# Feed-forwards: the low part of the inner activations is subtracted by GpSimd instead of VectorE

## The reference, cut to what matters

```python
def swiglu(h, w_gu, w_down):
    a, b = jnp.split(h @ w_gu, 2, axis=-1)
    return (jax.nn.silu(a) * b) @ w_down
# D_FF = 2816; per layer l:
x = x + 0.5 * mx[2] * swiglu(modulate(rms_norm(x, ...), mx[0], mx[1]), w_ffn1_gu[l], w_ffn1_down[l])
...
mx = jnp.split((silu_c @ w_ada[l] + b_ada[l])[:, None, :], 9, axis=-1)
```

## Time and profile before

| | |
|---|---|
| median of 3 runs | 2378.61 us (2377.94 to 2378.79) |
| profiled execution | 2378.87 us |
| its span, first to last instruction | 2377.1 us |
| mean granted TensorE clock in it | 0.985 of full speed |
| TensorE busy | 2289.9 us |
| VectorE busy | 1590.3 us |
| ScalarE busy | 887.6 us |
| GpSimd busy | 241.5 us |

### The profile page before, as it was taken

One profiled execution on the slowest core, in us unless ns is written; L12 is line 12 of the kernel. 1 busy time (PEld: TensorE's weight loads), 2 busy tenths in 40 slices (PEclk: granted clock), 3 DMA queues, 4 the chain that ended last, 5 costly groups with the idle time before them and its releaser, 6 DMA issues.

```text
span 2377.1 us, 33029 instructions
## 1 busy us (share of the span) xinstructions
PE 2289.9 (96%) x13198; PEld 1951.3 (82%) x13198; DVE 1590.3 (67%) x2898; ACT 887.6 (37%) x1507; POOL 241.5 (10%) x321
## 2 busy tenths in 40 slices
PE   6988989999999999999999999999999999998998
PEld 6878878988888777777888888888888898798998
DVE  5787886888877547875589866654333356876665
ACT  4444445422223444533322222332222234644443
POOL 1001012000102200012111111200000030021001
PEclk9999999999999999999999999999999999999999
DMA  7534534665643321222256565423222233254553
GB/s 264 168 126 159 169 126 143 217 217 174 221 172 123 116 69 65 67 84 98 91 195 240 201 212 205 140 80 107 93 94 98 93 111 105 98 170 141 188 184 119
DMA packets 97657, 341.31 MB, mean 144 GB/s; under 512 B 11312, under 2 KB 13488, under 8 KB 97120
## 3 DMA queue, kind: packets, MB, share of 16 engines
q1 hardware_dynamic: 74144, 254.46, 31.5%
q0 software_dynamic: 23360, 84.74, 11.0%
HBM read 338.11 MB, written 2.48 MB: 143 GB/s over the span
## 4 chain that ended last, share of the span: by engine, by line
PE 77%; DVE 13%; issue 4%; ACT 4%; POOL 1%; DMA 1%; POOLq 0%; DVEq 0%; ACTq 0%
PE PS L595 76%; DVE WL L1268 3%; ACT WH L965 1%; PE PS L916 1%; DVE NT L1277 1%; DVE HL L1277 1%; DVE JK L1278 1%; DVE AR L1278 1%; POOL ACC L1860 1%; ACT P L966 1%; DVE PJB L1277 1%; DVE CV L1277 1%; DMA RAW<-in_wst 0%; DVE P L1272 0%; POOL SS L1860 0%
## 5 line engine op out<-in xcount | busy, mean ns | idle before, releaser
L965 ACT ACTIVATE WH<-RAW 128x1024 fp32r<-128x1024 f32 (+3 forms) x498 | 511.5, 1028 | 977.3 <-PE PS L595 973.7
L595 PE MATMUL PS<-HH,WH 128*128 128x512 f32 (+1 forms) x2240 | 777.8, 347 | 11.1 <-DVE HL L1277 6.1
L595 PE MATMUL PS<-HL,WH 128*128 128x512 f32 (+1 forms) x2240 | 768.3, 343 | 0.0
L595 PE MATMUL PS<-HH,WL 128*128 128x512 f32 (+1 forms) x2240 | 768.1, 343 | 0.0
L1268 DVE TENSOR_TENSOR WL<-RAW,WH 128x1024 fp32r<-128x1024 f32 (+3 forms) x498 | 589.1, 1184 | 118.5 <-ACT WH L965 117.3
L595 PEld LDWEIGHTS PS<-HH,WH 128*128 128x128 f32 x2240 | 426.4, 190 | 74.4 <-DVE HL L1277 9.2
L595 PEld LDWEIGHTS PS<-HH,WL 128*128 128x128 f32 x2240 | 427.0, 191 | 52.5
L595 PEld LDWEIGHTS PS<-HL,WH 128*128 128x128 f32 x2240 | 427.3, 191 | 51.2
L595 PE MATMUL PS<-GH,WH 128*128 128x512 f32 (+1 forms) x776 | 271.2, 350 | 0.0
L595 PE MATMUL PS<-GL,WH 128*128 128x512 f32 (+1 forms) x776 | 270.2, 348 | 0.0
L595 PE MATMUL PS<-GH,WL 128*128 128x512 f32 (+1 forms) x776 | 270.1, 348 | 0.0
(11 more groups left out here) (220 smaller groups left out, 2791.6 us busy)
## 6 DMA issues: line engine op xcount, KB each, us to landing
RAW<-in_wst SPq DMA_DIRECT2D x436, 512.0 KB, 3.5
AR<-in_w_adaT POOLq DMA_DIRECT2D x144, 512.0 KB, 3.8
RAW<-in_wst SPq DMA_DIRECT2D x48, 384.0 KB, 3.0
BM<-rpb_rows POOLq DMA_DIRECT2D x48, 64.0 KB, 3.0
CB<-in_cc POOLq DMA_DIRECT2D x2, 1024.0 KB, 11.3
RAW<-in_wst SPq DMA_DIRECT2D x8, 256.0 KB, 2.7
RAW<-in_wst SPq DMA_DIRECT2D x4, 396.0 KB, 3.0
rpb_rows<-in_rpb POOLq DMA_DIRECT2D x2, 697.5 KB, 11.8
```

The lines of the kernel that those rows point to most:

```text
L595: return e.matmul(o, l, r, start=start, stop=stop)
L965: return e.activation(o, i, f, bias=bias, scale=scale)
```

## The change

VectorE's subtraction `GL = FT - GH` is taken out of its `evictions`, and GpSimd gets the same subtraction in its own, at the same place `V` of the list of steps. GpSimd waits there for ScalarE's rounding (`gh`). Those who waited for VectorE's signal `gl`, which are TensorE before the down products and ScalarE before the tanh of `ga`, now wait for GpSimd's. The whole diff:

```diff
@@ operand (TensorE)
             if un.buf == "G":
                 for s in halves:
-                    q.wait_ge(*vd.at("gl", l[0], PARTS[l[0]][l[1]][0] + kk, s))
+                    q.wait_ge(*gd.at("gl", l[0], PARTS[l[0]][l[1]][0] + kk, s))
@@ scalar_program, evictions, "ga"
                         if i >= 2:
                             for s in x.halves:
-                                q.wait_ge(*vd.at("gl", un.stage - 3, i - 2, s))
+                                q.wait_ge(*gd.at("gl", un.stage - 3, i - 2, s))
@@ vector_program, evictions, "gb"
                         stt(F, F, 0.5, P[:, 0:n], ALU.mult, ALU.mult).then_inc(*vd.inc("ev", d))
                         vd.same("gb", d)
-                        q.wait_ge(*ad.at("gh", d))
-                        tt(GL[:, slot(f, i), x.cols], F, GH[:, slot(f, i), x.cols].bitcast(f32), ALU.subtract).then_inc(
-                            *vd.inc("gl", f, i, x.halves[0]))
-                        vd.same("gl", f, i, x.halves[-1])
@@ pool_program, evictions
+                    elif x.kind == "gb":
+                        f = un.stage - 3
+                        q.wait_ge(*ad.at("gh", d))
+                        tt(GL[:, slot(f, i), x.cols], FT[:, i % 2, x.cols], GH[:, slot(f, i), x.cols].bitcast(f32),
+                           ALU.subtract).then_inc(*gd.inc("gl", f, i, x.halves[0]))
+                        gd.same("gl", f, i, x.halves[-1])
```

## The result

| | before | after |
|---|---|---|
| median | 2378.28 us (6 runs, 2376.19 to 2380.84) | 2393.33 us (6 runs, 2388.45 to 2395.25) |
| span of the profiled execution | 2377.1 us | 2393.5 us |
| mean granted clock in it | 0.985 | 0.981 |

The ratio is 1.0054, with a 95% interval of 1.0042 to 1.0067: 10 to 16 us slower. The median of after is 15 us higher. 2386.0 had been forecast, with 2377 to 2394 as range. So the sign was right and the range held, though by 0.7 us only, where single executions lie up to 5 us from their median; the size came out at about twice the forecast of 7.4 (15 us by the medians, 13 by the ratio).

A forecast was written before the change was run, and what follows sets the result against it. TensorE was taken as the bound, busy 2289.9 of 2377.1 us. Losses 3.3 + 4.8 + 0.8 + 2 + 1 = 11.9 less gain 4.5 gave +7.4 on 2378.9: 2386.3, for the median 2386.0, range 2377 to 2394.

The forecast's parts named there:

- What is removed: 98 subtractions leave VectorE; gain mainly from TensorE's waits at the start of f = 0, 4.5 us (1 to 8).
- Rival B: Faster: the waits of f = 0 vanish, the clock stays up, CB lands in time; 2372 us at best, chance 0.08.
- Price of a subtraction: On GpSimd a 512-column subtraction takes 1.28 us instead of 0.69, plus the rest of a VectorE operation already begun.
- Step 1: Start of f = 2: CB issued at 1186.8 behind a subtraction, landing at 1191.65, so ScalarE's tanh starts 3.4 us late.
- Steps 2 to 4: Start of f = 2: late CB delays VectorE, the first w_ada loads and a split; TensorE waits 3.3 us.
- the walk: The prediction's event-by-event trace of delays in f = 2, from the issue of CB to TensorE's waits.
- Step 5: First part of f = 2: rounds of GL, load, ada step and FT delay the sixth GL; TensorE waits 4.8 us (3 to 6).
- Step 6: Second part of f = 2: the same rounds average 11.1 us against TensorE's 11.2; wait 0.8 us (0 to 2), third part none.
- rival C: The circle of loads grows through the second and third part of f = 2; +19 us, 2398 us, chance 0.08.
- Step 7: The clock falls after TensorE's long waits in f = 2, costing 2 us (0 to 5).
- The other feed-forwards: f = 0, 3 and 5: later GL at ends of parts makes TensorE wait, 1 us in sum (0 to 2).

The follow-up runs named there:

- x8: Changed kernel, but only f = 0 has the subtraction on GpSimd, loads behind it; median 2379.1 us, ratio 0.9999 to the kernel before.
- x1: Changed kernel, but VectorE keeps the subtraction in f = 2; median 2380.7 us, ratio 1.0009 to the kernel before.
- x3: Changed kernel, all subtractions on GpSimd, but the next loads issued ahead of its wait for the rounding; median 2373.8 us, ratio 0.9985.
- x5: Changed kernel, but loads issued ahead of the subtractions at the start of f = 2 only; median 2384.1 us, ratio 1.0025.
- x7: As x3, but VectorE keeps the subtraction in f = 5; median 2372.9 us, ratio 0.9969 to the kernel before.
- x11: Changed kernel, but only f = 0 has the subtraction on GpSimd, with loads issued first; median 2376.0 us, ratio 0.9991.
- x2: Changed kernel, but only f = 2 has the subtraction on GpSimd; median 2396.6 us, ratio 1.0077 to the kernel before.
- x6: Changed kernel, but loads issued ahead of the subtractions everywhere except at the start of f = 2; median 2384.0 us, ratio 1.0015.
- x4: Changed kernel, but VectorE makes the subtractions and GpSimd only waits for the rounding, its DMAs behind that; median 2385.6 us, ratio 1.0031.
- x9: Changed kernel, but only the load of CB is issued ahead of a subtraction at the start of f = 2; median 2390.1 us, ratio 1.0056.
- x10: As x3, but each subtraction in f = 2 from the second inner tile on is made twice; median 2384.6 us, ratio 1.0030.

## Why the prediction was right or wrong

**What is removed: right in kind, too high.** Taken was a gain of 4.5 us (1 to 8). The waits at the start of f = 0 shrank from 4.55 to 1.79, the one at 433 vanished, the idle time in that stretch fell by 2.8, and by the marks the changed kernel stood 3.1 us ahead before f = 2. How much of the 3.1 is the change's own is open: the time up to the first wait of f = 0 runs from 406.0 to 412.3 over the thirteen profiled executions, and x8, with the change in f = 0 alone, shows no gain in its total. The fall of the clock after the first wait stayed (0.66 from 410 to 415 in both). Rival B needed it to go.

**Price of a subtraction: right.** With 512 columns GpSimd's took 1.26 to 1.34 us in 14 of 56 cases, which is the price of the row for the operation alone. It took 1.46 to 1.62 in 16 and 1.80 to 1.82 in 26, and I read what they have over 1.3 as GpSimd's own waiting for a VectorE operation that had begun. At the ends of parts in f = 3 the margin held.

**Step 1, CB: issue right, landing wrong.** GpSimd and the load at the start of f = 2, and its landing (DMA issues from 1150 to 1250), which answer to the earlier trace rows:

```profile
1182.20 1.47 POOL L1856 TENSOR_TENSOR GL<-FT,GH 128x256 fp32r<-128x256 f32 x1 [7.99 <-ACT GH L965]
1183.61 0.59 POOL L1956 DMA_DIRECT2D CB<-in_cc  x1
1197.94 1.29 POOL L1856 TENSOR_TENSOR GL<-FT,GH 128x512 fp32r<-128x512 f32 x1 [13.74 <-ACT GH L965]
1199.18 1.11 POOL L1950 DMA_DIRECT2D AR<-in_w_adaT  x2
```

```profile
CB<-in_cc POOLq DMA_DIRECT2D x1, 1024.0 KB, 7.6
```

Counted from the mark, it was issued at +21.3 (predicted 1186.8, +21.4). But the prediction kept the landing of 4.8 us, and it took 7.6. The versions that issue it early have 4.5 to 5.0 (x1, x3, x5 and x7 to x11), those that issue it six microseconds later, behind a subtraction, 7.6 to 7.9 (also x2, x6). Part of it may be the weight loads beside it: from issue to landing SyncE's queue moved 0.07 MB next to its 1.05 MB before, and 0.57 MB in the 7.6 us of after. But in x4, late and without a subtraction ahead, 0.79 MB were moved beside it and it took 6.0. The pieces of `w_ada` point the same way: from 1150 to 1250 their median was 3.8 us before and in x4, and 4.4 to 4.5 in the four versions that issue all or most of them right behind a subtraction (the changed kernel, x2, x5, x9). So that the late load takes longer is shown, and that it takes longest behind a subtraction; why is open. The prediction carried a landing time over to another moment without asking what else is moved then.

**Steps 2 to 4: one wait missed.** VectorE in after, which answers to the earlier trace rows:

```profile
1193.16 2.29 DVE L1277 SCALAR_TENSOR_TENSOR CB<-AR,CB 128x2048 f32<-128x2048 f32 x1 [7.78 <-ACT AR L965]
1195.37 1.22 DVE L1268 TENSOR_TENSOR WL<-RAW,WH 128x1024 fp32r<-128x1024 f32 x1
1196.50 0.68 DVE L1277 SCALAR_TENSOR_TENSOR FT<-FT,PS 128x512 f32<-128x512 f32 x1
1203.17 1.23 DVE L1278 SCALAR_TENSOR_TENSOR JK<-AR,CB 128x1024 bf16<-128x1024 f32 x1 [5.99 <-DMA AR<-in_w_adaT]
...
1205.47 1.22 DVE L1268 TENSOR_TENSOR WL<-RAW,WH 128x1024 fp32r<-128x1024 f32 x1
...
1248.41 0.68 DVE L1277 SCALAR_TENSOR_TENSOR FT<-FT,PS 128x512 f32<-128x512 f32 x1
1249.88 2.30 DVE L1278 SCALAR_TENSOR_TENSOR JK<-AR,CB 128x1024 bf16<-128x1024 f32 x1
```

FT of gb1 was foreseen at 1197.0 (it is 1196.5), the load at 1199.7 (1199.18), the first ada step at 1203.7 (1203.17), the split from 1206.0 (1205.47). But the walk named TensorE's wait for the second split only, 3.3 us. The split before it, at 1195.37, is late too: TensorE waits 2.03 for it. Together 6.32 in place of 3.3. The walk moved `CB` and its split and never asked when TensorE needs that split. The clock times agree, but the stage had begun 3.1 us earlier than the walk assumed: counted from the mark everything is late by the longer landing.

**Step 5, the circle: right, short by 3 us of 52.** From gb1 on, FT to FT was 16.4, 12.2, 13.8 and 9.5 us, against 16.4, 10.4, 12.8 and 9.1 foreseen: 51.9 against 48.7. Landings of the pieces went from 3.8 to 4.5 us (medians from 1150 to 1250). FT of the sixth tile came at 1248.41 (1245.8), `GL` ended at 1251.1 (1248.8), TensorE waited 4.61 (4.8): the extra 3 us of the circle were covered by the extra 3 us that TensorE had already waited. x5 and x6 show that circle and start each cost something by themselves.

**Step 6: too small.** The second part's wait is 3.22, for which 0.8 (0 to 2) stood. It went by averages, which don't hold the lengthened operations beside each subtraction. The third part has no wait over 0.4, as foreseen, so rival C is out.

**Step 7, clock: too small**, 5.1 us in f = 2 against 2, at the upper end of its 0 to 5. Both waits of over 4 us had the clock at half speed, as every one of 3.75 us or more has in the other versions' f = 2. Below that the length of a wait doesn't tell: at the 3.22 of after the clock stayed at 1.00 (1380 to 1390), at the 2.09 of x5 it fell (0.77 from 1365 to 1370).

**The other feed-forwards: 1 us foreseen.** f = 0 has a new wait of 0.85, f = 3 none over 0.4 for `GL`, f = 5 three, 1.89 together. Its stage took 201.9 to 203.1 us in the seven versions with GpSimd subtracting there, and 199.5 to 200.2 in the six without, so these waits are its cost of some 2 us; x7 takes them away. In the changed kernel it is 3.3, the rest a longer time at clock 0.50 behind the norm.

Sum of the errors: gain up to f = 2 too high by 1.4, start +3.0, first part -0.2, second part +2.4, clock and rest of f = 2 +2.4 (the 4.4 where 2 stood), f = 5 +2.3 (3.3 where 1 stood for three stages), stage of f = 3 -2.4. Of this last, half is the clock behind its norm (0.69 and 0.62 in the first windows of before) and half a matmul of 232.4 ns instead of 233.3, both chance as far as the runs tell. That is +8.9 on 7.4, or 16.3, against the 16.4 between the spans. It comes out by single executions, and chance terms of 1 to 2 us are in it.

**The range held in part by luck.** Its upper end counts 17 us of losses, while the bounds of its own terms add up to 3.3 + 6 + 2 + 5 + 2 = 18.3. And the start, the largest term after the first part, had no range at all: 3.3 stood in both ends, and 6.32 was measured.

## What to carry to other kernels

Before a wait is added to an idle engine, list the DMAs that stand behind it in its queue. Here a 1.3 us subtraction was harmless and a wait in front of the loads was not. The same work with the loads issued first turned 10 to 16 us of loss into a gain of 1 to 6 us (x3), and of 4.5 to 10 with VectorE keeping the subtraction in f = 5 (x7). And when a transfer moves, ask twice: when is it issued, and what else is being transferred then.

## What the runs showed of the hardware that I had not expected

- VectorE and GpSimd took turns by whole operations: 2.32, 2.31, then 1.21 us for the same kind of VectorE operation beside two subtractions of GpSimd (x10). VectorE's ada steps had means of 1385 and 1341 ns with GpSimd subtracting and 1218 and 1250 without (x4). Of 142 us that the change took off VectorE, 56.7 of it busy, the busy time shrank by 9.3.
- The load of 1 MB landed in 4.5 to 5.0 us or, issued 6 us later in the stage, in 7.6 to 7.9 behind a subtraction of GpSimd and in 6.0 without one (x4).
- Two things that cost 5.3 us and nothing in f = 2 alone (x4, x3) made 18.6 together, so what comes back when one part is undone is no share of the whole.
- A matmul of 512 columns took 233.3 ns through whole stages of some executions and 232.4 through the same stages of others: 430 matmuls in before and 432 in after, x1 and x3 from 1400 to 1500, at a granted clock of 1.00 in all. The runs don't tell why.
